# A block kernel on one Trainium2 core: in the first stage, half of each row's low parts is made on GpSimd instead of VectorE

## The reference

```python
ada = jax.nn.silu(c) @ w_ada[l] + b_ada[l]
shift_m, scale_m, gate_m, shift_f, scale_f, gate_f = [
    t[:, None, :] for t in jnp.split(ada, N_MOD, axis=-1)]
h = rms_norm(x, g_pre_mix[l]) * (1.0 + scale_m) + shift_m
z = h @ w_in[l]
...
x = x + gate_m * rms_norm(o, g_post_mix[l])
h = rms_norm(x, g_pre_ffn[l]) * (1.0 + scale_f) + shift_f
f = (jax.nn.silu(h @ w_ffn_gate[l]) * (h @ w_ffn_up[l])) @ w_ffn_down[l]
x = x + gate_f * rms_norm(f, g_post_ffn[l])
```

## Time and profile before

| what | value |
|---|---|
| runs | 2404.02 us median of 3 (2402.96 to 2410.23) |
| profiled execution, time | 2398.32 us |
| its span, first to last instruction | 2396.5 us |
| TensorE matmul, busy | 2299.6 us |
| VectorE, busy | 1533.6 us |
| ScalarE, busy | 1050.8 us |
| GpSimd, busy | 123.3 us |
| mean granted TensorE clock | 0.986 of full speed |

### The profile page before, as it was taken

How to read it: one execution, slowest core, us unless ns; L and a number is a source line. 1 busy time by engine, 2 the same in 40 slices (tenths; PEclk the granted TensorE clock), 3 DMA queues, 4 the chain that set the end, 5 groups by cost and what they waited for, 6 DMA issues and landing times.

```text
span 2396.5 us, 41646 instructions
## 1 busy us (share of the span) xinstructions
PE 2299.6 (96%) x16320; PEld 2150.4 (90%) x16320; DVE 1533.6 (64%) x1761; ACT 1050.8 (44%) x1246; POOL 123.3 (5%) x248
## 2 busy tenths in 40 slices
PE   3999989999999999999999999998999999999998
PEld 3899768899998899997899998798999988999986
DVE  7988789745544467754564898746565654566555
ACT  5463243644444334444553535645444443344443
POOL 0000012100001100001200000000000011000011
PEclk9999989999999999999999999899999999999999
DMA  9987949555555577865455453254555555555553
GB/s 396 422 349 308 359 157 389 200 186 190 181 190 193 193 260 268 284 215 184 160 178 175 158 177 121 71 177 141 180 185 183 188 193 193 188 181 187 181 193 123
DMA packets 163101, 506.47 MB, mean 211 GB/s; under 512 B 8112, under 2 KB 12512, under 8 KB 134320
## 3 DMA queue, kind: packets, MB, share of 16 engines
q1 hardware_dynamic: 161680, 500.28, 59.3%
q0 software_dynamic: 752, 3.48, 0.5%
q10 hardware_dynamic: 576, 1.44, 0.2%
HBM read 503.07 MB, written 2.10 MB: 211 GB/s over the span
## 4 chain that ended last, share of the span: by engine, by line
PE 87%; DVE 5%; DMA 4%; ACT 2%; issue 1%; POOL 0%; DVEq 0%; ACTq 0%; POOLq 0%; SPq 0%
PE pb L588 22%; PE pb L565 19%; PE pb L566 19%; PE pb L567 19%; DMA raw<-w_in 3%; PE pb L549 1%; PE pb L551 1%; PE pb L550 1%; PE pb L995 1%; PE pb L743 1%; DVE x L1736 1%; DMA sigc<-w_ada 1%; DVE wlo L512 1%; ACT xf L690 0%; DVE raw L477 0%
## 5 line engine op out<-in xcount | busy, mean ns | idle before, releaser
L455 DVE TENSOR_TENSOR wlo<-raw,whi 128x1024 fp32r<-128x1024 f32 (+1 forms) x704 | 854.0, 1222 | 714.1 <-ACT whi L448 712.6
L448 ACT ACTIVATE whi<-raw 128x1024 fp32r<-128x1024 f32 (+1 forms) x704 | 737.4, 1054 | 1043.3 <-PE pb L567 702.2
L565 PE MATMUL pb<-xh,whi 128*128 128x256 f32 (+2 forms) x3760 | 1063.2, 283 | 2.6 <-DVE wlo L455 1.9
L566 PE MATMUL pb<-xl,whi 128*128 128x256 f32 (+2 forms) x3760 | 1062.7, 283 | 0.0
L567 PE MATMUL pb<-xh,wlo 128*128 128x256 f32 (+2 forms) x3760 | 1061.6, 282 | 0.0
L565 PEld LDWEIGHTS pb<-xh,whi 128*128 128x128 f32 x3760 | 710.2, 189 | 3.5 <-DVE wlo L455 2.4
L566 PEld LDWEIGHTS pb<-xl,whi 128*128 128x128 f32 x3760 | 710.0, 189 | 0.0
L567 PEld LDWEIGHTS pb<-xh,wlo 128*128 128x128 f32 x3760 | 709.8, 189 | 0.0
L588 PE MATMUL pb<-whi,stg 128*128 128x512 f32 x1600 | 433.0, 391 | 7.2 <-DVE wlo L455 5.4
L588 PEld LDWEIGHTS pb<-whi,stg 128*128 128x128 f32 x1600 | 301.3, 189 | 73.8 <-issue 7.1
L588 PE MATMUL pb<-wlo,stg 128*128 128x512 f32 x800 | 247.9, 391 | 0.0
(11 more groups left out here) (390 smaller groups left out, 1656.5 us busy)
## 6 DMA issues: line engine op xcount, KB each, us to landing
raw<-w_ada SPq DMA_DIRECT2D x79, 1024.0 KB, 6.8
raw<-w_ffn_gate SPq DMA_DIRECT2D x44, 1024.0 KB, 5.2
raw<-w_ffn_up SPq DMA_DIRECT2D x44, 1024.0 KB, 5.2
raw<-w_ffn_down SPq DMA_DIRECT2D x44, 1024.0 KB, 4.7
raw<-w_gate SPq DMA_DIRECT2D x44, 1024.0 KB, 5.1
raw<-w_up SPq DMA_DIRECT2D x44, 1024.0 KB, 5.1
raw<-w_down SPq DMA_DIRECT2D x44, 1024.0 KB, 4.7
raw<-w_in SPq DMA_DIRECT2D x40, 1024.0 KB, 5.0
```

The lines of the kernel that those rows point to most:

```text
L448: act.activation(to, src, ACT.Copy).then_inc(hi_ready, 1)
L455: dve.tensor_tensor(to, src, hi, ALU.subtract).then_inc(raw_done, 1)
L565: mm(o, whi[:, s, t], xh[:, k, c0:c1], start=(k == 0), stop=False)
L566: mm(o, whi[:, s, t], xl[:, k, c0:c1], start=False, stop=False)
```

## The change

The second half of each row's `wlo` (128x1024) is made on GpSimd (`row_lo_second`), at the place in its queue behind the load of `wgu`. VectorE makes the first half only, and raises `raw_done` by two there. GpSimd counts its halves on `rows_done`, and TensorE waits for that count before the second half of a row. As a slot may be loaded again only when GpSimd has read it too, SyncE waits for `rows_done` as well wherever the unit that was in the slot is a row (`slot_read`). The later users of `rows_done` find 16 more on it, which `ROWS` allows for.

```diff
     def row_lo(k):
-        for hh, (s, src, n) in enumerate(row_halves(k)):
-            dve.wait_ge(hi_ready, W_WIN + 2 * k + hh + 1)
-            dve.tensor_tensor(wlo[:, s, 0:n], src, whi[:, s, 0:n].bitcast(F32), ALU.subtract).then_inc(raw_done, 1)
+        s, src, n = row_halves(k)[0]
+        dve.wait_ge(hi_ready, W_WIN + 2 * k + 1)
+        dve.tensor_tensor(wlo[:, s, 0:n], src, whi[:, s, 0:n].bitcast(F32), ALU.subtract).then_inc(raw_done, 2)
+
+    def row_lo_second(k):
+        s, src, n = row_halves(k)[1]
+        pool.wait_ge(hi_ready, W_WIN + 2 * k + 2)
+        pool.tensor_tensor(wlo[:, s, 0:n], src, whi[:, s, 0:n].bitcast(F32), ALU.subtract).then_inc(sem("rows_done"), 1)
+
+    def slot_read(n, u):
+        last = max(v for v in range(u) if FIRST_SLOT[v] == n) if n in FIRST_SLOT[:u] else None
+        if last is not None and FIRST[last][0] == "row":
+            sp.wait_ge(sem("rows_done"), FIRST[last][1] + 1)
...
-        pe.wait_ge(raw_done, done - 1)
+        pe.wait_ge(raw_done, done)
         for n in range(6):
...
-        pe.wait_ge(raw_done, done)
+        pe.wait_ge(sem("rows_done"), k + 1)
         for n in range(8, 16):
...
-    ROWS = {4: 1, (0, 0): 3, 5: 4, (1, 0): 6, 7: 7}
+    ROWS = {4: KT + 1, (0, 0): KT + 3, 5: KT + 4, (1, 0): KT + 6, 7: KT + 7}
...
             at_least(sp, raw_done, 2 * slot_before(u, slot))
+            slot_read(slot, u)
...
                     sp.wait_ge(raw_done, 2 * slot_before(u, u % RING))
+                    slot_read(u % RING, len(FIRST))
                     sp.dma_start(raw[:, u % RING, :], src).then_inc(landed[u % RING], 16)
...
         pool.dma_start(wgu[ROPE:ROPE + GRANK, :], a["w_gate_up"][0]).then_inc(sem("wgu_in"), 16)
+        for k in range(KT):
+            row_lo_second(k)
         pool.wait_ge(sem("kr_mm"), 1)
```

## The result

The changed kernel takes 2418.93 us (median of 6 runs, 2414.99 to 2423.82) against 2403.91 us for the kernel before, beside it: a ratio of 1.0062 with an interval of 1.0046 to 1.0078, so slower by 15.0 us. In a second comparison, `changed_again`, it was 2416.88 against 2402.48 us (1.0056, 1.0044 to 1.0068). Two executions are left out of all medians and ratios, one of `extra_full` (5332.55 us) and one of the kernel before beside `four_rows`, `filled_gaps` and `changed_again` (3260.06 us): their mean granted clock was 0.44 and 0.65.

A forecast was written before the change was run, and what follows sets the result against it. DMA engines bound the first stage (19.67 us per three rows), VectorE close behind at 19.1. Holds of 30.8 us less 16.0 saved and 2.5 idle give 12.3; 2404.0 + 12.3 = 2416 us, range 2405 to 2423.

The forecast's parts named there:

- The hold: First stage: GpSimd's subtraction stops VectorE's operations with two SBUF inputs for nearly its whole length, 2.05 us; chance 0.68.
- The step that decided: Carrying the casts' overlap over as a fixed part: a 2.30 us GpSimd subtraction stops VectorE 2.02 to 2.12 us, taken 2.05.
- The lower bound by share: VectorE stands 0.7 us per GpSimd subtraction if the casts' share 0.12 / 0.40 is what counts.
- the whole instruction: GpSimd's subtraction counted in full as hold on VectorE: the sum would end at 16.0 instead of 12.3 us.
- The sign that I named: VectorE's row sums beside GpSimd's subtractions at about 4.4 us instead of 2.35, or a gap of that size.
- The saving and the idle: First stage: VectorE saves 1.14 us per second half and has 2.5 us of idle over 14 rows to take up.
- the sum: Up to row 14: 30.8 us standing still, less 16.0 saved, less 2.5 idle taken up: 12.3 us later.
- rival 1: Part of the hold: GpSimd gives way within its instruction, VectorE stands 0.7 to 1.9 us, deciding at 1.32; chance 0.12.
- the clock's 1.6 us: Clock rival: TensorE's idle before row 14 lowers the granted clock, +1.6 us once; through whole rows +30 or more, chance 0.03.
- TensorE's second half: TensorE's wait for GpSimd's half of each row costs nothing, with 0.8 us of cover.
- lose their backlog: First stage: VectorE becomes the bound, so the DMA share from 60 to 130 us falls from 1.0 to about 0.9.
- TensorE's waits for `wlo`: In the first stage, TensorE's waits for VectorE's low halves rise from 8.7 to about 20 us.

The follow-up runs named there:

- `changed_again`: The changed kernel unaltered, run once more beside other runs on the same chip: 2416.88 us against 2402.48 us, ratio 1.0056.
- `extra_full`: The kernel before plus a GpSimd subtraction of 128x1024 per row of w_in, which nobody waits for in the stage: 2434.04 us, ratio 1.0123.
- `four_rows`: The changed kernel with only the second halves of rows 0, 4, 8 and 12 on GpSimd, the others on VectorE: 2403.21 us, ratio 1.0004.
- `filled_gaps`: The changed kernel plus 7 matmuls of a zero tile on TensorE before rows 4, 7, 8, 11, 13 and 14: 2413.05 us, ratio 1.0051.
- `extra_half`: The kernel before plus a GpSimd subtraction of 128x512 per row of w_in, which nobody waits for in the stage: 2415.21 us, ratio 1.0056.
- `extra_writes`: The kernel before plus two GpSimd memsets of 128x1024 per row, which read nothing: 2400.71 us, ratio 0.9992.
- `saved_only`: The changed kernel without GpSimd's subtractions of rows 2 to 15, so their second halves' low parts are stale: 2402.41 us, ratio 0.9999.

## Why the prediction was right

**The hold.** The step that decided, 2.05 us per subtraction carried over from casts of 0.40 us, was right in kind and a little small: 2.13 us in the changed kernel, 2.16 alone, 1.01 at half the size. That it came so near has some luck in it: the casts gave 0.12 to 0.22 us of 0.40, and that the rest is a fixed part, and not a share, was a choice which only `extra_half` bears out. The lower bound by share (0.7 us) was wrong, the size goes with the columns. With 2.3 us, the whole instruction, it would have been 16.0 us for row 14, by the casts 12.3, measured 13.7: between the two. The first is what the rule of the Trainium skill gives (SBUF — State Buffer, section "SBUF: two separate sides"). The same page of the Trainium skill states, in the section "Who interferes with whom", that VectorE with two SBUF inputs contends with a GpSimd instruction that reads SBUF, not with one that only writes it; `extra_writes` agrees, for memsets. That VectorE would go free with one input in SBUF, no run here tries. The sign that I named, row sums of about 4.4 us, came only where a row sum stood next; most often it was an `xl` of 2.64.

**The saving and the idle.** 1.14 us saved per row and 2.5 us of idle stand: VectorE's idle fell from 2.48 to 0.12 us. One number beside the sum was off. With the 15 holds that the sum counts, rival 1 decides at (14 x 1.14 + 2.5) / 15 = 1.23 us and not at 1.32; nothing else hangs on it. That the saving is worth nothing by itself is shown by `saved_only`.

**Carried to the end.** Row 14: 13.7 us for 12.3. The chunks: 15.2 for 12.3, as the clock's 1.6 us, which I had as a rival only, came true before row 14 (1.5 us, gone in `filled_gaps`). The medians are 15.0 us apart. The forecast of 2416 us is 2.9 us below the measured time: 1.4 of it is the hold, 1.5 the clock. Of the next stage's 2.3 us, 1.2 to 1.6 stand in kernels that are no slower too, so most of it lies in the one execution of the kernel before that all are laid beside. The rest can't be told from noise: the interval of the ratio is 11 to 19 us.

**TensorE's second half** costs nothing, as said: TensorE never waited for GpSimd, and `extra_full` loses its time in a kernel that has no such wait.

**What failed.** I wrote that the DMA engines "lose their backlog", that their share from 60 to 130 us would be about 0.9, and even that the prediction is wrong if it stays at 1.0. It stayed at 1.01. The error is in turning a rate over three rows into a share of that window. A load stands 16.25 us in the queue, and VectorE is late by 13.7 us only at the end; so the lateness first eats the backlog, and the DMA engines go on at full rate until the loads of the stage are nearly in. What was missing from their share came afterwards, the stretch at 0.00 from 139.2 to 150 us. `extra_full`, whose lateness grows past 16.25 us, shows the fall that I forecast, in the same window:

```profile
60.00:130.00 70.00, 54.52 (x403) 53.28 (x401) 70.00 (x50) 24.38 (x32) 27.10 (x9) 0.90 0.93 363
```

The sum over the stage was not touched by it, as VectorE's queue is what it was made from. TensorE's waits for `wlo` came to 16.2 us where I had about 20. About 3 us of the lateness went into rows 4 and 8, which ran some 1.5 us slower each after the clock's falls, and no longer stood as waiting.

## What to carry to other kernels

Before work goes from VectorE to an idle GpSimd, count inputs: where GpSimd's instruction reads SBUF and VectorE's have two inputs there, the two took turns here, and by the sum the move pays only if GpSimd's time is shorter than VectorE's own for the same work (here 2.13 us of standing for 1.14 saved). What falls into VectorE's idle costs less, as in `four_rows`. Ask also what the relieved engine is worth: a kernel that leaves the moved work out altogether, as `saved_only`, gives the most that any such move can bring, here nothing. And a queue that is some 16 us deep hides about as much lateness from the share of the engine behind it: it stayed at 1.01 in the kernel that was 13.7 us late at row 14, and was 0.93 in the one that was 29.9 us late.

## What the runs showed of the hardware

- A subtraction of 128x1024 on GpSimd stops VectorE for 2.13 to 2.16 us, one of 128x512 for 1.01; two memsets of 1.97 us together stop it for nothing. The stopped time is written into VectorE's instruction (`xl` 2.64 us for 0.42), so busy time can rise when work is taken away: 1546.8 us for 1533.6, with 16 instructions fewer.
- Gaps of 1.9 to 2.4 us at TensorE were at times enough for the granted clock to fall to 0.60 over the next 4 us (before rows 4, 8 and 14), and at times not (before rows 7, 11 and 13, gaps of 2.3 us). In `changed_again`, the same kernel, the fall before row 11 came too. In `filled_gaps` one came at 170.0 with no wait over 0.23 us in the 16 us before it.
